# Cached attention in a hybrid decoder step: VectorE adds a page's scores ahead of, not behind, the low part of the page two later

## The chip, the cores and the metric

One NeuronCore of one Trainium2 chip runs the whole program. The metric is the device time of one execution in microseconds (us); the figure given for a kernel is the median of its runs.

## The reference

One inference step of a two-layer trunk, in float32: layer 0 is multi-head latent attention followed by a gated MLP, layer 1 is an S5 state-space layer followed by the same kind of MLP. The change lies in layer 0, in the attention of eight sample sequences with four new tokens each over a paged cache of 4096 positions (32 cache pages of 128 rows for each sequence):

```python
def one_sequence(a):
    pt, q1, c1, r1 = a
    c_all = jnp.concatenate([ckv_pool[pt].reshape(past, KV_LORA).astype(c1.dtype), c1], axis=0)
    r_all = jnp.concatenate([kpe_pool[pt].reshape(past, QK_ROPE).astype(r1.dtype), r1], axis=0)
    k, v = mla_keys_values(c_all, r_all, *kv_w)
    return causal_attend(q1, k, v, q_pos, k_pos)
```

`mla_keys_values` multiplies a latent row (256 numbers) by `w_kv_up` for 8 heads, puts the shared rotary key beside each head's 64 numbers and divides each head's key by its root mean square. `causal_attend` is a softmax attention with scale 96 ** -0.5.

## The kernel before

The program runs one stage after another: projections, attention of the prompt, attention over the cache (`attend_cache`, some 535 us), output projection, then the MLP, the S5 layer and the second MLP. Each stage is a block in which every engine has its own written-out instruction stream, and semaphores order them. An engine takes its instructions strictly in the order in which they are written here, so the place of an instruction in the stream is the subject of this case.

In `attend_cache` the unit of work is one cache page: `b` counts sequences (0 to 7), `p` pages of a sequence (0 to 31), `n = 32 b + p` pages in all. Sequences 0, 1, 6 and 7 are written out with constants, sequences 2 to 5 run in a loop, where `b` lives in a register and semaphore targets are worked out from it. The products must keep float32 accuracy, so a page's transposed latent is split into a high part (`cT_hi`, rounded) and a low part (`cT_lo`, the rest), and three products replace one. For a page n the engines do:

- TensorE: `turn_page` (L1307) transposes page n + 1 into the buffer `tc`; then the page's twelve matmuls (L1343 and L1345) into `kn`, which hold the keys of all heads and, in the last 32 columns, the unscaled scores. `tc`, `kn`, `cT_hi`, `cT_lo` and `sq` have two buffers each, taken in turn. In the twelve matmuls the latent is the stationary operand, so a weight load of `cT_hi` or `cT_lo` comes before each. Before the twelve, TensorE waits for `cl_done` (`cT_lo` of page n is there), `sq_done` and `s_kept` (both of page n - 2: its `kn` buffer has been read by ScalarE and by VectorE). Behind the pages with p % 4 == 1 it transposes the rotary keys of the next group of four pages (L1317), behind those with p % 4 == 3 it makes their scores (L1322).
- ScalarE: `hi` (L1428) copies `tc` of page n, rounded, into `cT_hi`; then `squares` (L1435) squares the keys of page n - 2 out of `kn`; at some pages also a copy of the rotary scores (L1444), of the rotary keys (L1455), or a square root for a group (L1462).
- VectorE: `lo` (L1536) subtracts `cT_hi` from `tc` of page n into `cT_lo`; then `sums` of page n - 2: the add of its scores (L1545) and the sum of its squares (L1546); at p % 4 == 1 and 3 also the work on a finished group of four pages (L1567; L1573, L1577, L1579). Once for each sequence come further operations of the softmax (L1596 to L1622).

The helper `behind` gives a function page p - 2, or one of the last two pages of the sequence before.

Of the kernel before, what the change touches and what calls it, by code (L numbers as in the profile page):

```python
# [573 lines left out]
NG = DM // GC  # L574
# [515 lines left out]
def attend_cache(nc, io, consts, keep, o_new, w_out):  # L1090
# [12 lines left out]
    GP = 4  # L1103
    EP = (NPAGE + 1) // 3
    NG = NPAGE // GP
# [3 lines left out]
    with ExitStack() as ctx:  # L1109
# [6 lines left out]
        def sem(name):  # L1116
            return ctx.enter_context(nc.semaphore("ca_" + name))
# [68 lines left out]
        sr_kept = sem("sr_kept")  # L1186
# [32 lines left out]
        def stream(b, page, at):  # L1219

            for p in range(NPAGE):
                if not isinstance(b, int) or b < NSEQ:
                    page(b, p)
                if p in at:
                    at[p](b)

        def behind(work, b, p):

            if p >= 2:
                work(b, p - 2)  # L1230
            elif not isinstance(b, int) or b > 0:
                work(b - 1, NPAGE - 2 + p)
# [260 lines left out]
        def _(dve):  # L1493
# [30 lines left out]
            def put_queries(b):  # L1524

                if not isinstance(b, int) or b >= 2:
                    dve.wait_ge(page_done, (b - 1) * NPAGE)
                nc.vector.tensor_copy(wb_hi[:, b % 2, :, HALF:], qc[:, :, b, :]).then_inc(q_put, 1)
                nc.vector.tensor_tensor(wb_lo[:, b % 2, :, HALF:], qc[:, :, b, :], qc_hi[:, :, b, :], ALU.subtract).then_inc(q_put, 1)

            def lo(b, p):
                n = b * NPAGE + p
                dve.wait_ge(ch_done, n + 1)
                if not isinstance(n, int) or n >= 2:
                    dve.wait_ge(page_done, n - 1)
                nc.vector.tensor_tensor(cT_lo[:, p % 2, :], tc[:, p % 2, 0:KVL], cT_hi[:, p % 2, :], ALU.subtract).then_inc(cl_done, 1)  # L1536

            def sums(b, p):
                n = b * NPAGE + p
                g = b * NG + p // GP  # L1540
                dve.wait_ge(sq_done, n + 1)

                dve.wait_ge(sr_kept, g + 1)
                cur = scores[:, b % 2, p, :]
                nc.vector.tensor_tensor(cur, cur, kn[:, p % 2, 1, HALF:HALF + QC], ALU.add).then_inc(s_kept, 1)  # L1545
                nc.vector.tensor_reduce(ssum[:, b % 2, p, :], sq[:, p % 2, :].rearrange("p (h d) -> p h d", h=H),  # L1546
                                        AXX, ALU.add).then_inc(ss_done, 1)
                if p % GP == 0:

                    dve.wait_ge(kpe_sqd, g + 1)  # L1550
                    nc.vector.tensor_reduce(ssum_pe[:, b % 2, p:p + GP], kpe_sq[:, p // GP % RG, :, :], AXX, ALU.add).then_inc(kpe_ss, 1)

            def page(b, p):
                if p == 0:
                    put_queries(b)
                lo(b, p)
                behind(sums, b, p)
                if p % GP == 1 and p > GP:
                    group_square(b, p // GP - 1)
                if p % GP == 3 and p > GP:  # L1560
                    scale_group(b, p // GP - 1)

            def group_square(b, g):

                own = slice(g * GP, (g + 1) * GP)
                dve.drain()
                nc.vector.tensor_tensor(rms[:, 0, g % 2, :, :], ssum[:, b % 2, own, :],  # L1567
                                        ssum_pe[:, b % 2, own].unsqueeze(2).to_broadcast([P, GP, H]), ALU.add).then_inc(ms_done, 1)

            def scale_group(b, g):  # L1570

                dve.wait_ge(sd_done, b * NG + g + 1)
                nc.vector.reciprocal(rms[:, 2, g % 2, :, :], rms[:, 1, g % 2, :, :])  # L1573
                dve.drain()
                cur = scores[:, b % 2, g * GP:(g + 1) * GP, :]
                flat = cur.rearrange("p g (h t) -> p (g h) t", h=H)
                nc.vector.tensor_tensor(flat, flat, rms[:, 2, g % 2, :, :].rearrange("p g h -> p (g h)").unsqueeze(2).to_broadcast([P, GP * H, NDEC]), ALU.mult)  # L1577
                dve.drain()
                nc.vector.tensor_reduce(tops[:, g, :], cur.rearrange("p g c -> p c g"), AXX, ALU.max)  # L1579
# [25 lines left out]
            def shift(b, part):  # L1605
                if in_range(b, 1, NSEQ):
                    dve.wait_ge(top_spread, b)
                    own = slice(0, NPAGE // 2) if part == 0 else slice(NPAGE // 2, NPAGE + 1)
                    cur = scores[:, (b - 1) % 2, own, :]
                    nc.vector.tensor_tensor(cur, cur, misc[:, 0:QC].unsqueeze(1).to_broadcast([P, own.stop - own.start, QC]), ALU.subtract).then_inc(shifted, 1)  # L1610
# [12 lines left out]

            def step(b):
                if isinstance(b, int) and b == NSEQ:
                    behind(sums, b, 0)
                    behind(sums, b, 1)
                stream(b, page, {1: begin, 3: last_group, 4: mean, 5: column_top, 9: row_top,
                                 12: lambda b: shift(b, 0), 13: lambda b: shift(b, 1)})

            sequences(dve, step)
            dve.wait_ge(o_done, 1)
            nc.vector.tensor_copy(o_new[:, :], kn[0:TS, 0, 0, :]).then_inc(o_kept, 1)
# [1661 lines left out]
```

## Time and profile before

| | |
|---|---|
| median of 3 runs | 3077.82 us |
| range of the runs | 3076.28 to 3091.57 us |
| the profiled execution | 3089.39 us |
| its span, first to last instruction | 3087.6 us |
| mean granted TensorE clock, share of full | 0.975 |
| TensorE busy (matmuls) | 2940.7 us, 95% of the span |
| VectorE busy | 1871.4 us, 61% |
| ScalarE busy | 968.2 us, 31% |
| first matmuls of the cached stage, its first and last page | 434.3 and 962.2 us |

The profile records one execution. PE is TensorE's matmuls, PEld its weight loads, which overlap the matmuls; DVE is VectorE, ACT ScalarE, POOL GpSimd. A row's line number is that of the code above. "Idle before" is the time that an engine stood still right ahead of an instruction, with the instruction whose semaphore ended it. Busy shares over the whole span mix stages with different limits; the cached stage is about a sixth of it.

### The profile page before, as it was taken

How to read it: one execution, taken by the hardware profiler on the slowest of the kernel's cores; microseconds unless marked ns; L12 is line 12 of the kernel's file. 1: busy time of each engine (PE TensorE's matmuls, PEld its weight loads, DVE VectorE, ACT ScalarE, POOL GpSimd, SP SyncE). 2: the span in 40 equal slices, each digit the busy share in tenths (PEclk: the TensorE clock that was granted, in tenths of full speed). 3: DMA queues.
4: the chain of work that ended last, by engine and by line, in shares of the span. 5: the costliest groups of instructions: out<-in, count | busy, mean ns of one | idle time of the engine just before them, and what ended most of it. 6: DMA issues, size and time to landing. Idle time of an engine off the chain costs nothing. (4 is left out here: it accounts for less than half of the span.)

```text
span 3087.6 us, 54484 instructions
## 1 busy us (share of the span) xinstructions
PE 2940.7 (95%) x19232; PEld 2756.5 (89%) x19232; DVE 1871.4 (61%) x3827; ACT 968.2 (31%) x1739; POOL 266.9 (9%) x352
## 2 busy tenths in 40 slices
PE   8979889999998999999999998999989999999998
PEld 5646679998996899999999987989989999999998
DVE  3436667777775465656665675882346556666565
ACT  3433345555554322222222232222222222222221
POOL 1003300000000000000000007650000000000000
PEclk9988999999998999999999998989999999999999
DMA  3010013222221021111111124334111111111111
GB/s 110 28 23 1 35 45 82 73 75 70 74 75 46 28 62 42 41 49 46 48 41 54 35 73 116 80 105 126 42 51 60 44 41 43 52 48 41 54 34 69
DMA packets 262263, 174.37 MB, mean 56 GB/s; under 512 B 77977, under 2 KB 247658, under 8 KB 261818
## 3 DMA queue, kind: packets, MB, share of 16 engines
q1 hardware_dynamic: 261882, 171.85, 19.3%
q8 instruction: 102, 1.67, 0.2%
q14 instruction: 87, 0.71, 0.1%
q10 hardware_dynamic: 192, 0.13, 0.0%
HBM read 149.49 MB, written 22.29 MB: 56 GB/s over the span
## 5 line engine op out<-in xcount | busy, mean ns | idle before, releaser
L1641 PE MATMUL f_up<-h_hi,f_wu_hi 128*128 128x352 f32 x2112 | 459.8, 326 | 16.8 <-DVE h_lo L2145 15.1
L1641 PE MATMUL f_up<-h_hi,f_wu_lo 128*128 128x352 f32 x2112 | 457.1, 324 | 0.0
L1641 PE MATMUL f_up<-h_lo,f_wu_hi 128*128 128x352 f32 x2112 | 456.9, 325 | 0.0
L1641 PEld LDWEIGHTS f_up<-h_hi,f_wu_hi 128*128 128x128 f32 x2112 | 361.2, 190 | 18.0 <-issue 15.7
L1641 PEld LDWEIGHTS f_up<-h_hi,f_wu_lo 128*128 128x128 f32 x2112 | 364.5, 189 | 0.0
L1641 PEld LDWEIGHTS f_up<-h_lo,f_wu_hi 128*128 128x128 f32 x2112 | 360.6, 189 | 0.0
L2053 ACT ACTIVATE f_conv<-f_u_row,f_taps 128x1056 f32<-128x1056 f32 x88 | 111.8, 1271 | 774.2 <-DVE f_u_row L2175 774.2
L2244 DVE TENSOR_TENSOR resid<-resid,f_down 128x352 f32<-128x352 f32 x528 | 271.3, 518 | 107.2 <-PE f_down L1999 104.1
L2175 DVE TENSOR_TENSOR f_u_row<-f_up,inv 128x1056 f32<-128x1056 f32 x88 | 110.5, 1256 | 345.0 <-PE f_up L1641 331.9
L1999 PE MATMUL f_down<-f_a_hi,f_wd_hi 128*128 (+1 forms) x960 | 317.1, 330 | 1.1 <-DVE resid L2244 0.5
L1999 PE MATMUL f_down<-f_a_hi,f_wd_lo 128*128 (+1 forms) x960 | 309.7, 323 | 0.0
L1999 PE MATMUL f_down<-f_a_lo,f_wd_hi 128*128 (+1 forms) x960 | 309.3, 322 | 0.0
L1999 PEld LDWEIGHTS f_down<-f_a_hi,f_wd_hi 128*128 128x128 f32 x960 | 180.3, 188 | 16.4 <-DVE resid L2244 9.1
L2191 DVE SCALAR_TENSOR_TENSOR f_conv<-f_u_row,f_taps,f_conv 128x512 f32<-128x512 f32 x176 | 126.0, 748 | 106.4 <-ACT f_u_new L2055 106.4
L1999 PEld LDWEIGHTS f_down<-f_a_lo,f_wd_hi 128*128 128x128 f32 x960 | 181.0, 188 | 0.0
L1999 PEld LDWEIGHTS f_down<-f_a_hi,f_wd_lo 128*128 128x128 f32 x960 | 180.6, 188 | 0.0
L1546 DVE TENSOR_REDUCE ca_ssum<-ca_sq 128x8 f32<-128x512 f32 x256 | 173.7, 678 | 0.0
L1343 PE MATMUL ca_kn<-ca_wa_hi,ca_cT_hi 128*128 128x256 f32 x512 | 158.0, 324 | 14.3 <-DVE ca_scores L1545 14.3
L1536 DVE TENSOR_TENSOR ca_cT_lo<-ca_tc,ca_cT_hi 128x256 fp32r<-128x256 f32 x256 | 107.8, 421 | 97.3 <-ACT ca_cT_hi L1428 93.3
L1435 ACT ACTIVATE ca_sq<-ca_kn 128x512 f32<-128x512 f32 x256 | 152.6, 596 | 1.5 <-PE ca_kn L1345 1.5
L1345 PE MATMUL ca_kn<-ca_wb_hi,ca_cT_lo 128*128 128x288 f32 x512 | 140.9, 298 | 0.0
L1428 ACT ACTIVATE ca_cT_hi<-ca_tc 128x256 fp32r<-128x256 f32 x256 | 97.7, 382 | 137.8 <-PE ca_tc L1307 134.8
(428 smaller groups left out, 5628.1 us busy)
## 6 DMA issues: line engine op xcount, KB each, us to landing
f_wu<-ffn_w_up SPq DMA_DIRECT2D x86, 512.0 KB, 4.0
ca_cache<-cache_ckv SPq DMA_DIRECT2D x256, 128.0 KB, 2.0
raw<-ffn_w_down SPq DMA_DIRECT2D x44, 512.0 KB, 4.2
raw<-ssm_w_out SPq DMA_DIRECT2D x16, 512.0 KB, 3.8
s_spill<-resid SPq DMA_DIRECT2D x8, 528.0 KB, 10.7
s_u<-sm_ut SPq DMA_DIRECT2D x8, 528.0 KB, 2.7
resid<-s_spill SPq DMA_DIRECT2D x8, 528.0 KB, 8.5
pj_xb<-x_prompt SPq DMA_DIRECT2D x8, 512.0 KB, 3.6
```

Of the source, the lines that this page charges most:

```text
L1343: nc.tensor.matmul(kn[:, p % 2, 0, 0:HALF], c[:, p % 2, k * P:(k + 1) * P], wa[:, k, :], start=(x == 0 and k == 0), stop=(x == 2 and k == ...
L1345: mm = nc.tensor.matmul(kn[:, p % 2, 1, 0:HALF + QC], c[:, p % 2, k * P:(k + 1) * P], wb[:, s, k, :], start=(x == 0 and k == 0), stop=(x = ...
L1428: nc.scalar.activation(cT_hi[:, p % 2, :], tc[:, p % 2, 0:KVL], ACT.Copy).then_inc(ch_done, 1)
L1435: nc.scalar.activation(sq[:, p % 2, :].rearrange("p (a c) -> p a c", a=2), kn[:, p % 2, :, 0:HALF], ACT.Square).then_inc(sq_done, 1)
L1536: nc.vector.tensor_tensor(cT_lo[:, p % 2, :], tc[:, p % 2, 0:KVL], cT_hi[:, p % 2, :], ALU.subtract).then_inc(cl_done, 1)
L1546: nc.vector.tensor_reduce(ssum[:, b % 2, p, :], sq[:, p % 2, :].rearrange("p (h d) -> p h d", h=H), AXX, ALU.add).then_inc(ss_done, 1)
L1641: mm = nc.tensor.matmul(out(c), w, x(c), start=(first and n == 0), stop=(last and n == 2))
L1999: mm = nc.tensor.matmul(down[:, x % 2, 0:CH], w[:, jj, m * P:(m + 1) * P], a[:, chunk(c)], start=(jj == 0 and q == 0), stop=(jj == GJ - 1 ...
L2053: nc.scalar.activation(conv[:, half, :], u_row[:, half, 2:], ACT.Identity, bias=taps[:, 3, bass.ds(t, 1)], scale=taps[:, 2, bass.ds(t, 1)])
L2175: nc.vector.tensor_tensor(u_row[:, half, 2:].rearrange("p (c n) -> p c n", c=NCH), up[:, half, :, 0:CH], inv[:, :].rearrange("p (c n) -> p ...
L2191: nc.vector.scalar_tensor_tensor(out=c[:, own], in0=u_row[:, half, own.start + 1:own.stop + 1], scalar=w[1], in1=c[:, own], op0=ALU.mult, ...
L2244: nc.vector.tensor_tensor(cur, cur, down[:, x % 2, 0:CH], ALU.add).then_inc(added, 1)
```

## The change

`sums` is cut in two. Its first half, the wait for the squares and for the rotary scores and the add of the scores, becomes `latent_scores`, which `page` calls for page p - 2 ahead of `lo` for page p. The rest of `sums` stays behind `lo`. Behind the last page the two halves run for each of the two pages left. No operation is added or taken away and no semaphore changes its meaning.

```diff
-            def sums(b, p):
+            def latent_scores(b, p):
                 n = b * NPAGE + p
-                g = b * NG + p // GP
                 dve.wait_ge(sq_done, n + 1)
-
-                dve.wait_ge(sr_kept, g + 1)
+                dve.wait_ge(sr_kept, b * NG + p // GP + 1)
                 cur = scores[:, b % 2, p, :]
                 nc.vector.tensor_tensor(cur, cur, kn[:, p % 2, 1, HALF:HALF + QC], ALU.add).then_inc(s_kept, 1)
+
+            def sums(b, p):
+                g = b * NG + p // GP
                 nc.vector.tensor_reduce(ssum[:, b % 2, p, :], sq[:, p % 2, :].rearrange("p (h d) -> p h d", h=H),
                                         AXX, ALU.add).then_inc(ss_done, 1)
                 if p % GP == 0:
@@ -1553,6 +1554,7 @@
             def page(b, p):
                 if p == 0:
                     put_queries(b)
+                behind(latent_scores, b, p)
                 lo(b, p)
                 behind(sums, b, p)
                 if p % GP == 1 and p > GP:
@@ -1623,8 +1625,9 @@
             def step(b):
                 if isinstance(b, int) and b == NSEQ:
-                    behind(sums, b, 0)
-                    behind(sums, b, 1)
+                    for p in range(2):
+                        behind(latent_scores, b, p)
+                        behind(sums, b, p)
```

## Rows read from the trace of the kernel before

**Rows 1.** The stage's middle, by stretches: busy us of each engine, clock, DMA share

```profile
core 0: us, PE busy (x) PEld busy (x) DVE busy (x) ACT busy (x) POOL busy (x), PEclk, DMA share, GB/s
...
620.00:680.00 60.00, 58.20 (x499) 54.88 (x498) 45.94 (x135) 33.28 (x86) 2.94 (x7) 1.00 0.28 71
```

**Rows 2.** Who waited for whom, TensorE, 434 to 970 us: total, times, longest

```profile
PEld ca_kn L1343 <- DVE ca_cT_lo L1536: 15.8, 18, 1.3
...
PE ca_kn L1343 <- DVE ca_scores L1545: 14.3, 22, 1.2
```

**Rows 3.** Groups by line, 434 to 970 us: busy, mean ns, idle before

```profile
L1536 DVE TENSOR_TENSOR ca_cT_lo<-ca_tc,ca_cT_hi 128x256 fp32r<-128x256 f32 x256 | 107.8, 421 | 97.3 <-ACT ca_cT_hi L1428 93.3
...
L1428 ACT ACTIVATE ca_cT_hi<-ca_tc 128x256 fp32r<-128x256 f32 x255 | 97.3, 382 | 137.8 <-PE ca_tc L1307 134.8 <-issue 2.1
```

**Rows 4.** Timeline around page 23 of sequence 3: start, duration

```profile
675.93 0.37 ACT L1428 ACTIVATE ca_cT_hi<-ca_tc 128x256 fp32r<-128x256 f32 x1
...
676.19 0.60 ACT L1435 ACTIVATE ca_sq<-ca_kn 128x512 f32<-128x512 f32 x1
...
676.34 0.42 DVE L1536 TENSOR_TENSOR ca_cT_lo<-ca_tc,ca_cT_hi 128x256 fp32r<-128x256 f32 x1 [0.43 <-ACT ca_cT_hi L1428]
...
676.83 0.19 DVE L1545 TENSOR_TENSOR ca_scores<-ca_scores,ca_kn 128x32 f32<-128x32 f32 x1
...
676.93 0.68 DVE L1546 TENSOR_REDUCE ca_ssum<-ca_sq 128x8 f32<-128x512 f32 x1
676.95 0.26 PEld L1307 LDWEIGHTS ca_tc<-ident,ca_cache 128*128 128x128 f32 x2
...
677.17 0.19 PEld L1343 LDWEIGHTS ca_kn<-ca_wa_hi,ca_cT_hi 128*128 128x128 f32 x1
```

**Rows 5.** The same timeline, on to page 24 of the sequence

```profile
677.53 0.34 DVE L1573 RECIPROCAL ca_rms<-ca_rms 128x32 f32<-128x32 f32 x1
...
678.31 0.39 DVE L1579 TENSOR_REDUCE ca_tops<-ca_scores 128x32 f32<-128x128 f32 x1
...
678.62 0.41 DVE L1536 TENSOR_TENSOR ca_cT_lo<-ca_tc,ca_cT_hi 128x256 fp32r<-128x256 f32 x1
...
678.95 0.17 DVE L1545 TENSOR_TENSOR ca_scores<-ca_scores,ca_kn 128x32 f32<-128x32 f32 x1
...
679.24 0.19 PEld L1343 LDWEIGHTS ca_kn<-ca_wa_hi,ca_cT_hi 128*128 128x128 f32 x1
```

**Rows 6.** The same timeline, on to page 25 of the sequence

```profile
679.70 0.59 ACT L1435 ACTIVATE ca_sq<-ca_kn 128x512 f32<-128x512 f32 x1
...
680.97 0.19 PEld L1343 LDWEIGHTS ca_kn<-ca_wa_hi,ca_cT_hi 128*128 128x128 f32 x1
```

**Rows 7.** Timeline at page 19 of sequence 3, behind ScalarE's work on exponentials and root

```profile
664.56 0.59 ACT L1435 ACTIVATE ca_sq<-ca_kn 128x512 f32<-128x512 f32 x1
...
665.18 0.19 DVE L1545 TENSOR_TENSOR ca_scores<-ca_scores,ca_kn 128x32 f32<-128x32 f32 x1
...
665.48 0.19 PEld L1343 LDWEIGHTS ca_kn<-ca_wa_hi,ca_cT_hi 128*128 128x128 f32 x1 [1.33 <-DVE ca_cT_lo L1536]
```

**Rows 8.** Squares and add at page 22 of sequence 3 (in the loop)

```profile
674.21 0.59 ACT L1435 ACTIVATE ca_sq<-ca_kn 128x512 f32<-128x512 f32 x1
...
674.92 0.19 DVE L1545 TENSOR_TENSOR ca_scores<-ca_scores,ca_kn 128x32 f32<-128x32 f32 x1 [0.15 <-ACT ca_sq L1435]
```

**Rows 9.** The same pair at page 18 of sequence 6 (written out)

```profile
865.64 0.59 ACT L1435 ACTIVATE ca_sq<-ca_kn 128x512 f32<-128x512 f32 x1
...
866.27 0.19 DVE L1545 TENSOR_TENSOR ca_scores<-ca_scores,ca_kn 128x32 f32<-128x32 f32 x1
```

**Rows 10.** Stretches around the one fall of the clock inside the stage

```profile
691.00:697.60 6.60, 3.36 (x26) 2.89 (x24) 3.06 (x11) 2.45 (x7) 0.40 (x1) 0.91 0.30 82
697.60:704.40 6.80, 6.57 (x34) 6.58 (x34) 3.64 (x12) 1.39 (x5) 0.00 (x0) 0.59 0.32 85
704.40:720.00 15.60, 15.60 (x131) 15.58 (x130) 13.29 (x40) 8.94 (x25) 0.80 (x2) 1.00 0.22 58
```

## The prediction

> **What bounds the kernel now.** I read the page's busy line first (TensorE's matmuls fill 95% of the span), then the stretches, waits and groups of the cached stage alone, and last its timeline page by page, since the change moves one small instruction by one place. In 60 us of the stage's middle TensorE's matmuls are busy for 58.20 us at the full clock and VectorE for 45.94 us [rows 1]: TensorE sets the pace and VectorE has about a quarter of its time free, but not at every moment. What counts is the moment at which a cache page's twelve matmuls may start. I take it from the weight load L1343 that opens them.
>
> The waits of TensorE [rows 2] name two things: the weight load stood 15.8 us for `cT_lo` and the matmul 14.3 us for `ca_scores`. These are the same pauses seen on two queues. The timeline tells which of the two came last: at page 23 of sequence 3 the low part had ended at 676.76, the add ended at 677.02, the weight load began at 677.17 [rows 4]; at page 24 the add ended at 679.12 and the load began 0.12 later at 679.24 [rows 5]; at page 19 it is 665.37 and 665.48, 0.11 later [rows 7]. So where TensorE waits today it waits for the add, the later of VectorE's two instructions, and 0.11 us is the way from such an end to the load. At page 23 it did not wait: its transposes (from 676.95, 0.26) had only just ended.
>
> The second thing to see is what VectorE waits for. Ahead of `lo` it stands 97.3 us in all, 93.3 of them for `cT_hi` [rows 3]. Ahead of the add it hardly stands, because `lo` fills the time. On ScalarE `hi` of page n comes first and `squares` of page n - 2 right behind it: 675.93 and 676.19, ending at 676.30 and 676.79 [rows 4]. The squares therefore end about 0.49 us after the high part, and the add starts 0.04 after them (676.83), or 0.03 at page 19 [rows 4, 7]. `lo` of page 23 started at 676.34, 0.04 after its high part, while the squares were still running.
>
> **The change part by part.** It adds and removes no operation and issues no transfer. It moves one add of 0.19 us (256 of them) ahead of `lo` and with it the wait for the squares. Behind that waiting instruction now stand `lo` of page n, the reduction of page n - 2 and all group work; for `lo` waits TensorE. No other queue is passed: SyncE's loads wait for `page_done` and have a DMA share of 0.28 to move in [rows 1], POOL's squares of the rotary keys wait for nothing that moves.
>
> *A page whose add waits for the squares.* Two consecutive VectorE instructions start closer than the first one's duration: add to the next 0.10 (676.83 to 676.93) [rows 4], `lo` to the next 0.33 (678.62 to 678.95) [rows 5]. The new order at page 23: add at 676.83 as before, `lo` 0.10 later at 676.93, its end 0.42 later at 677.35, the weight load 0.11 later at 677.46 instead of 677.17 [rows 4]: 0.29 us late. In short, the load can start no sooner than 0.67 after the squares' end (0.04 + 0.10 + 0.42 + 0.11), where it was 0.38 after. At page 19, where ScalarE is late, the load moves from 665.48 to 665.18 + 0.63 = 665.81, 0.33 late [rows 7].
>
> *The next page, with the group's work on VectorE.* The reduction now starts 0.33 behind `lo`, at 677.26 instead of 676.93, 0.33 late. From there to `lo` of page 24 it was 1.69 us of work without a gap (676.93 to 678.62) [rows 4, 5]. The new order has the add at 678.95, `lo` at 679.05, its end (0.41) at 679.46, the load 0.11 later at 679.57 instead of 679.24: 0.33 late in all, so this page adds 0.04. Where VectorE is behind anyway, the swap itself costs 0.01: `lo` then add took 0.50 from start to end, add then `lo` takes 0.51.
>
> *The page after it.* Page 25's squares ended at 680.29 and its load began at 680.97, 0.68 after [rows 6]. That is just the 0.67 needed, and ScalarE's squares move by 0.29 with the matmuls of page 23 while the load moves by 0.33, so nothing is added. The pages with p % 4 == 2 may be held up by about 0.1, but the page behind them is held more and by a chain that starts one page earlier (its high part is made from a transpose issued ahead of the wait), so the larger of the two counts, not the sum.
>
> *The sum.* One group of four pages loses 0.33 us. There are 8 groups in a sequence and 8 sequences: 64 x 0.33 = 21.1 us. The groups are not all alike. Behind exponentials the wait is the 0.33 of page 19; some groups have more room. I take 0.33 as the mean.
>
> *The loop.* In sequences 2 to 5 a wait's target is worked out in a register first. Where a new value is wanted right at the add, the add starts late: squares' end 674.80, add 674.92, 0.12 after [rows 8], against 866.23 and 866.27, 0.04 after, at the written-out sequence 6 [rows 9]. Today `lo`'s own targets are worked out while the reduction runs. In the new order they stand between a waiting add and `lo`, with nothing to cover them. No row shows this; from below it costs nothing, from above the step of rows 8 once or twice (0.08 to 0.16) on each held page. I take 0.12 for each group: 4 sequences x 8 groups x 0.12 = 4 us.
>
> The forecast is 21 + 4 = 25 us. Against the profiled execution that is 3089.4 + 25 = 3114 us; that execution lies 12 us above the median of the runs, and the difference carries over: 3077.8 + 25 = 3103 us.
>
> *The bounds.* From below: if a quarter of the groups have the room and the page behind adds nothing, 48 x 0.29 = 14 us. From above: if the reduction had to wait for all of `lo` (0.42 instead of 0.33), 64 x 0.09 = 6 us more; if the register step is also paid in the written-out sequences, 4 more; if pages with p % 4 == 1, which have 0.01 to spare, pay the step in full, 0.1 x 64 = 6 more: 41 us.
>
> *A rule weighed.* Rows 4 show the reduction starting 0.10 behind an add that lasts 0.19. The Trainium skill, page "VectorE: DVE Perf Modes", section "The DRAIN you can't avoid", says that the next operation does not start until the pipeline has emptied; a later section ("Two Vector instructions with no wait between them") says that one that is not held starts earlier. By the first, `lo` would start 0.19 behind the add and the reduction 0.42 behind `lo`, 0.09 more at both places: 0.18 x 64 = 11.5 us on top, 3115 us. The trace agrees with the second, and the sum goes by its rows.
>
> **The rivals.**
> - *Hidden (no change).* The whole stage has DVE and ACT idle time, and VectorE's order could be free. For it: only 22 waits for the add are recorded, so most pages have some room. Against it: the room is 0.15 us between the add's end and the load at page 23 [rows 4], of which 0.11 is the way itself, and the new end lies 0.33 later than the old one. It would need the squares to end 0.3 us sooner. A half-size version (only pages with late squares lose, many groups have room) gives 10 to 15 us, 3088 to 3093 us, inside what can be told from no change.
> - *Faster.* `s_kept` comes sooner at pages where VectorE is behind, such as page 24: the add would end at 678.62 + 0.17 instead of 679.12 [rows 5]. If that were the gate and `lo` were not needed at once, all waits for the add would go: 14.3 us [rows 2], 3063 us. It decides only if the first weight load could start without `lo`; but the twelve matmuls wait for both ahead of the first load, and `lo` ends later by the same work.
> - *The clock.* TensorE has more short pauses. The one fall inside the stage came behind a stretch with 3.36 us busy of 6.60 [rows 10]; the pause of 1.33 us at page 19 [rows 7] lies in a stretch with the clock at full [rows 1]. In the fall's 6.80 us 34 matmuls ran, where at full clock 131 took 15.60 [rows 10], so 57 would have run: 23 x 0.119 = 2.7 us lost. If the pauses, now up to 1.33 + 0.33, cause one such fall in each of 7 sequences, 19 us come on top: 3122 us. The Trainium skill, page "TensorE: Matmul & The Clock Gate", section "A second HAM failure mode: psum-queue depth-cycling", says that frequent small pauses between matmul groups can make the clock swing; no row here shows that for pauses of this size.
> - *VectorE falls behind for good.* If the idle time ahead of the add plus group work exceeded a page's period, delays would add up: 0.1 us on each of 256 pages gives 26 us on top, 3129 us. Against it: page 25 shows VectorE back on time.
>
> **How the numbers follow.** A measurement of this kernel tells from no change what is over about 0.5%, 15 us. Chances: forecast mechanism at its size or near (18 to 40 us slower) 0.70; half-size or hidden 0.18; clock 0.05; falling behind 0.03; faster 0.04. The likeliest one's own range is 3093 to 3119 us. To hold 8 in 10, the range goes from 3085 (part of the half-size cases) to 3122 (the clock's case). Slower by over 0.5%: 0.70 + 0.05 + 0.03 = 0.78; within 0.5%: 0.19; faster 0.03, since that case reaches only 14.3 us.
>
> **What would show it.** In the profile after: VectorE's idle time ahead of `lo` for `cT_hi` is nearly gone, and an idle time of the same order or more (100 to 140 us) stands ahead of the add, ended by `ca_sq`; TensorE waits for `ca_cT_lo` ahead of L1343 and no longer for `ca_scores`, some 100 times or more and some 50 us in total; the load of L1343 starts 0.67 after the squares' end at pages 3, 7, ..., 31, and 0.1 to 0.2 more in sequences 2 to 5. The stage from 434.3 to 962.2 us grows by 25 us and the other stages by nothing. It would be wrong if squares end relatively sooner than now, if the clock falls more often in the stage, or if pages with p % 4 == 1 and 2 are held as well.

## The result and the profile after

The changed kernel takes 3104.81 us (median of 8 runs, 3099.72 to 3109.75) against 3079.61 us (8 runs, 3074.77 to 3091.57) for the one before. The ratio is 1.0081, with a 95% interval of 1.0067 to 1.0094: 0.81% slower, 21 to 29 us. The profiled execution took 3109.75 us, its span is 3107.9 us.

The stage itself can be told more closely than the whole. From the first to the last page's opening weight load it lasts 548.7 us (433.9 to 982.6) instead of 527.9 (434.3 to 962.2): 20.8 us more. What is left of the span is 2559.2 us after and 2559.7 before, so in this pair nothing else moved. Over the twelve executions profiled in this case, the rest of the span lies anywhere from 2539.7 to 2559.7 us although its code is the same; that spread, and not the stage, makes the medians uneven. It goes with the mean granted clock of the execution: the shortest rest, 2539.7 us, has 0.982, the longest, 2559.7 us, 0.975. For each kernel below both numbers are given, and the stage is what its explanation goes by. Each stage figure is one profiled execution against the one of the kernel before (527.9 us); the change, profiled a second time in a later session, gave 21.8 us instead of 20.8, so a difference of 1 us between such figures tells nothing.

Who waited for whom in the changed kernel, 434 to 1000 us; total, times, longest:

```profile
PEld ca_kn L1343 <- DVE ca_cT_lo L1536: 24.1, 48, 1.6
...
DVE ca_scores L1543 <- ACT ca_sq L1435: 134.7, 174, 5.0
...
DVE ca_cT_lo L1536 <- ACT ca_cT_hi L1428: 1.1, 1, 1.1
```

VectorE's idle time has changed its place. It stood 93.3 us for the high part ahead of `lo` [rows 3]; now that is 1.1 us, and 134.7 us stand ahead of the add, for the squares. TensorE's matmul waits of 14.3 us for the scores [rows 2] are gone from the list; what it waits for is the low part (its matmuls 15.2 us).

Page 23 of sequence 3 in the changed kernel, the counterpart of [rows 4]:

```profile
685.04 0.37 ACT L1428 ACTIVATE ca_cT_hi<-ca_tc 128x256 fp32r<-128x256 f32 x1
...
685.31 0.60 ACT L1435 ACTIVATE ca_sq<-ca_kn 128x512 f32<-128x512 f32 x1
...
685.94 0.19 DVE L1543 TENSOR_TENSOR ca_scores<-ca_scores,ca_kn 128x32 f32<-128x32 f32 x1 [0.51 <-ACT ca_sq L1435]
...
686.10 0.42 DVE L1536 TENSOR_TENSOR ca_cT_lo<-ca_tc,ca_cT_hi 128x256 fp32r<-128x256 f32 x1
...
686.20 0.26 PEld L1307 LDWEIGHTS ca_tc<-ident,ca_cache 128*128 128x128 f32 x2
686.45 0.67 DVE L1547 TENSOR_REDUCE ca_ssum<-ca_sq 128x8 f32<-128x512 f32 x1
686.58 0.19 PEld L1343 LDWEIGHTS ca_kn<-ca_wa_hi,ca_cT_hi 128*128 128x128 f32 x1
```

The high part ends at 685.41, as early as ever, but `lo` starts at 686.10. The squares end at 685.91, the add starts 0.03 later, `lo` 0.16 after the add, and it ends at 686.52; TensorE is through with its transposes by 686.46 and begins only at 686.58.

The same page of sequence 6, which is written out with constants and not in the loop:

```profile
898.33 0.60 ACT L1435 ACTIVATE ca_sq<-ca_kn 128x512 f32<-128x512 f32 x1
898.96 0.19 DVE L1543 TENSOR_TENSOR ca_scores<-ca_scores,ca_kn 128x32 f32<-128x32 f32 x1 [0.68 <-ACT ca_sq L1435]
899.07 0.42 DVE L1536 TENSOR_TENSOR ca_cT_lo<-ca_tc,ca_cT_hi 128x256 fp32r<-128x256 f32 x1
...
899.54 0.19 PEld L1343 LDWEIGHTS ca_kn<-ca_wa_hi,ca_cT_hi 128*128 128x128 f32 x1 [0.19 <-DVE ca_cT_lo L1536]
```

Here `lo` starts 0.11 behind the add, and the load 0.61 behind the squares' end (898.93) instead of 0.67. From `lo`'s end to the load it is 0.05.

The growth by sequence, from the starts of the pages' opening weight loads (from the last page of the sequence before to its own last page), after minus before, in us:

| sequence | 0 | 1 | 2 | 3 | 4 | 5 | 6 | 7 |
|---|---|---|---|---|---|---|---|---|
| | 2.05 | 2.05 | 3.41 | 3.03 | 3.03 | 3.23 | 2.00 | 2.02 |

The written-out sequences lose 2.03 us each, those in the loop 3.18. By a page's place in its group of four, the period that ends with a page of p % 4 == 3 has 11.8 us of the growth, p % 4 == 0 3.3, p % 4 == 2 4.1 (3.6 of them in the loop) and p % 4 == 1 1.5.

### The profile page after: what moved, and what is told of

The parts are those of the page before. It is cut to its first block and busy times, and to the rows that moved or that the text cites. A ratio compares the mean times of both kernels' runs of the same rounds, so it can differ in the third digit from the quotient of the medians.

```text
span 3107.9 us, 54484 instructions
## 1 busy us (share of the span) xinstructions
PE 2958.4 (95%) x19232; PEld 2759.2 (89%) x19232; DVE 1865.0 (60%) x3827; ACT 968.9 (31%) x1739; POOL 266.1 (9%) x352
## 5 line engine op out<-in xcount | busy, mean ns | idle before, releaser
L1644 PE MATMUL f_up<-h_hi,f_wu_hi 128*128 128x352 f32 x2112 | 459.6, 326 | 16.8 <-DVE h_lo L2148 15.2
L1343 PE MATMUL ca_kn<-ca_wa_hi,ca_cT_hi 128*128 128x256 f32 x512 | 162.0, 331 | 15.8 <-DVE ca_cT_lo L1536 15.2
L1345 PE MATMUL ca_kn<-ca_wb_lo,ca_cT_hi 128*128 128x288 f32 x512 | 140.8, 297 | 0.0
```

Of the source, the lines that this page charges most:

```text
L1343: nc.tensor.matmul(kn[:, p % 2, 0, 0:HALF], c[:, p % 2, k * P:(k + 1) * P], wa[:, k, :], start=(x == 0 and k == 0), stop=(x == 2 and k == ...
L1345: mm = nc.tensor.matmul(kn[:, p % 2, 1, 0:HALF + QC], c[:, p % 2, k * P:(k + 1) * P], wb[:, s, k, :], start=(x == 0 and k == 0), stop=(x = ...
L1644: mm = nc.tensor.matmul(out(c), w, x(c), start=(first and n == 0), stop=(last and n == 2))
```

## The experiments

Each kernel was timed in five rounds beside the kernel before, on the same chip as that one. There were three such sessions, each on a chip of its own: e1 to e4; e5 to e8; the change again and e9. Ratios are to the kernel before of the same session; stages are all compared with the 527.9 us above.

**Where the loss sits: e1_new_at_3 and e2_new_but_3.** The new order at one page in four, then at the other three:

```diff
# e1_new_at_3
-                behind(latent_scores, b, p)
+                if p % GP == 3:
+                    behind(latent_scores, b, p)
                 lo(b, p)
+                if p % GP != 3:
+                    behind(latent_scores, b, p)
                 behind(sums, b, p)
# e2_new_but_3: the same with == and != exchanged
```

> The new order at the pages with p % 4 == 3 alone, the old order at the other three in four. Theory of the prediction (the low part now stands behind an add that waits for the squares, and the pages whose squares end late have no room): these pages and the group pages behind them carried 12.3 + 3.3 us of the change's 20.8 us in the stage, and some of what the loop's p % 4 == 2 pages took comes back to them, so 15 to 19 us slower than before. Rival, that the new order costs about the same at every page: a quarter, 5 to 7 us.

> The new order at all pages but those with p % 4 == 3. Theory of the prediction: only page 16 of a sequence (0.28 us late, 7 times) and, in the looped sequences, the pages that are held by the register step (about 0.12 at each p % 4 == 2) lose, 6 to 9 us slower than before. Rival of an even cost: three quarters, 16 to 19 us.

(The 12.3 us in the expectation of e1 should read 11.8.) e1 measured 1.0057 (1.0043 to 1.0070), 18 us, stage + 19.4 us, a little over its band. e2 measured 1.0014 (1.0005 to 1.0023), 4 us, stage + 5.4 us. One page in four carries nearly the whole loss; the even split (5 to 7 and 16 to 19 us) falls. e2 came out under its band (6 to 9 us) by time and by stage. In it, page 16 is 0.17 late in written-out sequences and 0.25 in the loop, where 0.28 had been written down. That the two add up to more than the change (24.8 against 20.8 us) is also as it should be: a page held at p % 4 == 2 costs nothing where the page behind is held anyway.

**Wait or place: e3_wait_alone.** The old order of operations, with one wait more:

```diff
+                behind(squares_made, b, p)     # dve.wait_ge(sq_done, n + 1) of that page
                 lo(b, p)
                 behind(sums, b, p)
```

> The old order of the operations, and one more wait: VectorE waits for the squares of page n - 2 ahead of the low part of page n. Nothing else moves. Theory of the prediction: it is the wait and not the place of the add that costs, so the time is about that of the change, 18 to 30 us slower than before, and TensorE waits for the add, about 0.6 to 0.7 us after the squares' end. Rival, that the add's own 0.10 us ahead of the low part, or another order of writes, is what costs: no change, within 5 us of before.

1.0093 (1.0079 to 1.0106), 29 us, stage + 29.0 us. Page 23 of sequence 6:

```profile
906.42 0.60 ACT L1435 ACTIVATE ca_sq<-ca_kn 128x512 f32<-128x512 f32 x1
907.05 0.42 DVE L1539 TENSOR_TENSOR ca_cT_lo<-ca_tc,ca_cT_hi 128x256 fp32r<-128x256 f32 x1 [0.68 <-ACT ca_sq L1435]
...
907.39 0.17 DVE L1548 TENSOR_TENSOR ca_scores<-ca_scores,ca_kn 128x32 f32<-128x32 f32 x1
...
907.68 0.19 PEld L1343 LDWEIGHTS ca_kn<-ca_wa_hi,ca_cT_hi 128*128 128x128 f32 x1 [0.23 <-DVE ca_cT_lo L1539]
```

No operation has been moved, and the loss is all there. `lo` starts 0.03 behind the squares' end (907.02), the add ends at 907.56, the load comes 0.12 later, 0.66 behind the squares. (The row puts the pause down to `cT_lo`, which had ended at 907.47; the add was the last.) The wait is the cause. The add's place is even the better one once the wait stands: the way from the squares' end to the load is 0.05 longer here than in the changed kernel.

The 29.0 us are not the price of the wait alone, though. The written-out sequences lose 2.67 us each (2.03 in the changed kernel), the looped ones 4.59 (3.18). Page 23 of sequence 3, in the loop:

```profile
689.72 0.60 ACT L1435 ACTIVATE ca_sq<-ca_kn 128x512 f32<-128x512 f32 x1
690.51 0.42 DVE L1539 TENSOR_TENSOR ca_cT_lo<-ca_tc,ca_cT_hi 128x256 fp32r<-128x256 f32 x1 [0.68 <-ACT ca_sq L1435]
...
691.14 0.19 PEld L1343 LDWEIGHTS ca_kn<-ca_wa_hi,ca_cT_hi 128*128 128x128 f32 x1 [0.23 <-DVE ca_cT_lo L1539]
```

Here `lo` starts 0.19 behind the squares' end (690.32) and the load 0.82 behind it, so the added wait brings 0.16 more in the loop. The clean comparison is that of the written-out sequences.

**The loop's surplus: e4_targets_first and e9_squares_named_first.** In e4 both waits of `lo` are put ahead of the add's two waits, so that nothing is left to do between a waiting add and `lo`; ScalarE makes the high part before the squares in any case.

```diff
# e4_targets_first
+                lo_ready(b, p)          # lo's waits: ch_done n + 1, page_done n - 1
                 behind(latent_scores, b, p)
                 lo(b, p)                # without waits
# e9_squares_named_first, on top of e4: the wait for sq_done ahead of lo_ready
+                behind(squares_made, b, p)
                 lo_ready(b, p)
                 behind(latent_scores, b, p)   # with the wait for sr_kept alone
```

> The change, with the low part's own two waits (high part made, matmuls of page n - 2 done) put ahead of the add's waits, so that in the looped sequences nothing is worked out between a waiting add and the low part. Theory: the looped sequences lose 3.07 us each and the written-out ones 2.1; with this they lose alike, 3 to 4.5 us less than the change, 20 to 22 us slower than before, and the low part starts 0.10 after the add everywhere. Rival, that the loop's surplus comes from something else: the time of the change, 24 to 26 us slower.

1.0099 (1.0084 to 1.0115), 31 us: slower than the change, not faster. Stage + 33.7 us. Half of the theory holds and half does not. The sequences now lose alike (4.6, 4.0, 4.6, 4.2, 4.2, 4.4, 3.8, 3.9 us), and `lo` starts 0.10 to 0.11 behind the add everywhere, so what stood between a waiting add and `lo` did make the surplus at the held pages. What is left of it, 0.3 us a sequence, lies at the first page of a looped sequence. But the level is that of the loop's sequences and more, 2 us over the change in each written-out one, because the add itself starts late:

```profile
908.53 0.60 ACT L1435 ACTIVATE ca_sq<-ca_kn 128x512 f32<-128x512 f32 x1
909.33 0.19 DVE L1545 TENSOR_TENSOR ca_scores<-ca_scores,ca_kn 128x32 f32<-128x32 f32 x1 [0.68 <-ACT ca_sq L1435]
```

The squares end at 909.13 and the add starts 0.20 later, at the same page where it was 0.03 in the changed kernel. The new theory was that the order in which the waits are written decides which of them travels with the instruction.

> The change itself once more, so that the next kernel can be compared with it on the same chip: 22 to 28 us slower than before.

> The low part's waits ahead of the add, as in e4, but the wait for the squares is written first of all of them. In e4 the add started 0.20 after the squares' end instead of 0.03. Theory: only the first wait written ahead of an instruction travels with it, the others are steps of the engine's sequencer that cost some 0.17 once the late one is through; with the squares written first the add starts 0.03 to 0.05 after them again, the low part 0.10 after the add in the looped sequences too, and the time is 3 to 5 us under the change, 20 to 22 us slower than before. Rival, that the number of waits costs whatever their order: as e4, 30 us slower.

On the third chip the change measured 1.0067 (1.0050 to 1.0084), 21 us and so just under its band of 22 to 28, with a stage of + 21.8 us, and e9 1.0071 (1.0045 to 1.0098), 22 us (14 to 30), with + 27.2 us. By time the two can't be told apart, and e9's lies in its band; by the stage e9 is 5.4 us worse than the change and 6.5 better than e4 (on another chip), and that misses the band. By sequence e9 lost 2.4, 2.1, 4.7, 4.6, 4.6, 4.5, 2.3, 2.0 us. Page 23 of sequence 3 (loop), then that of sequence 6 (written out), both of e9:

```profile
690.83 0.60 ACT L1435 ACTIVATE ca_sq<-ca_kn 128x512 f32<-128x512 f32 x1
691.65 0.19 DVE L1546 TENSOR_TENSOR ca_scores<-ca_scores,ca_kn 128x32 f32<-128x32 f32 x1 [0.62 <-ACT ca_sq L1435]
691.75 0.42 DVE L1538 TENSOR_TENSOR ca_cT_lo<-ca_tc,ca_cT_hi 128x256 fp32r<-128x256 f32 x1
...
907.37 0.60 ACT L1435 ACTIVATE ca_sq<-ca_kn 128x512 f32<-128x512 f32 x1
908.00 0.19 DVE L1546 TENSOR_TENSOR ca_scores<-ca_scores,ca_kn 128x32 f32<-128x32 f32 x1 [0.68 <-ACT ca_sq L1435]
908.11 0.42 DVE L1538 TENSOR_TENSOR ca_cT_lo<-ca_tc,ca_cT_hi 128x256 fp32r<-128x256 f32 x1
```

Written out, the add starts 0.03 behind the squares (907.97, 908.00) although four waits stand ahead of it, two of them those of `lo`: the order in which the waits are written is what counts, not their number, and the rival falls for these sequences. In the loop it starts 0.22 behind (691.43, 691.65), and the forecast of an even loss fails there. The likely reason is that in the loop the next thing behind the first-named wait is not the add but the step that works out a target in a register, and that this step takes the wait; that is inferred from the starts (`lo` in e3 starts 0.19 instead of 0.03 behind in the same way) and was not tried by itself. An order that is good in both kinds of sequence stays unfound.

**ScalarE's order: e5_squares_first, e6_squares_first_old and e7_mixed.** The squares end late because ScalarE makes the high part first. Here that is turned round, under the new order on VectorE (e5), under the old one (e6), and, with the new order, everywhere but at the pages with p % 4 == 3, which keep the old order on both engines (e7).

```diff
# e5_squares_first (on the change), e6_squares_first_old (on the kernel before)
-                hi(b, p)
                 behind(squares, b, p)
+                hi(b, p)
# e7_mixed: squares first and scores first if p % GP != 3, both behind hi and lo if p % GP == 3
```

> The change, and ScalarE squares page n - 2 ahead of the high part of page n (it did the reverse). The add then waits for squares that end early, and the low part for a high part that starts some 0.05 later at most pages, since the squares fill the time of the transposes. Theory: the chain squares, add, low part is cut; only the pages with p % 4 == 3 and page 16 lose, where the high part is late already (it moves by 0.49, the load by about 0.12), and the group page behind adds 0.05: 9 to 14 us slower than before, about half of the change. Rival, that ScalarE's order does not matter and the add's place does: 24 to 26 us slower.

> The kernel before, and ScalarE squares first, as a control: with the old order on VectorE the load needs the high part, the low part and the add in turn. Theory: at p % 4 == 3 the high part is 0.49 later, the add then ends 0.50 after the low part's start, the load comes about 0.25 to 0.3 late: 16 to 24 us slower than before, more than with the new order on VectorE. Rival, that whichever order ScalarE takes is free: within 5 us of before.

> Squares first on ScalarE and the add first on VectorE, but both in the old order at the pages with p % 4 == 3. Theory: every page then has its chain inside its period; page 16 is 0.17 late in seven sequences; 0 to 4 us slower than before, hardly to be told from it. Rival, that the add ahead of the low part costs by itself: 8 us slower or more (three quarters of the pages carry it).

| | ratio | interval | stage |
|---|---|---|---|
| e5 | 1.0036 | 1.0023 to 1.0050 | + 11.1 us |
| e6 | 1.0062 | 1.0049 to 1.0075 | + 19.0 us |
| e7 | 0.9993 | 0.9984 to 1.0002 | + 0.1 us |

All three lie in their bands by the stage (e7's time even lies 2 us under the kernel before, not to be told from it). Page 23 of sequence 3 in e5:

```profile
677.34 0.59 ACT L1435 ACTIVATE ca_sq<-ca_kn 128x512 f32<-128x512 f32 x1
...
677.82 0.38 ACT L1428 ACTIVATE ca_cT_hi<-ca_tc 128x256 fp32r<-128x256 f32 x1
...
677.96 0.19 DVE L1543 TENSOR_TENSOR ca_scores<-ca_scores,ca_kn 128x32 f32<-128x32 f32 x1 [0.99 <-ACT ca_sq L1435]
...
678.23 0.42 DVE L1536 TENSOR_TENSOR ca_cT_lo<-ca_tc,ca_cT_hi 128x256 fp32r<-128x256 f32 x1
...
678.71 0.19 PEld L1343 LDWEIGHTS ca_kn<-ca_wa_hi,ca_cT_hi 128*128 128x128 f32 x1
```

Now the add has its squares at 677.93, ahead of the high part (678.20), and `lo` follows the high part by 0.03: the chain is cut. What is left is the high part's own delay of 0.48 by the squares, which a page of this kind has no room for. Its load comes 0.12 late in e5 and 0.28 in e6 at most pages with p % 4 == 3 that had none to spare (0.17 and 0.34 at page 19). At those pages the looped sequences lose what the written-out ones lose, save at page 31 (0.17 against 0.12): an add that does not wait hides the register step, which bears out from the other side what the loop's surplus was. e7 shows the add ahead of `lo` at three pages in four with no loss at any but page 16 (0.17, as written down) and the first page of a looped sequence (0.13 to 0.25), and a gain of 0.05 to 0.07 at pages 20, 24 and 28. So the add's new place costs next to nothing where ScalarE squares first. ScalarE's mixed order with the old order on VectorE was not tried, so e7 doesn't tell what the add's place gives or takes by itself.

**A faster kernel: e8_pair_early.** On the kernel before:

```diff
# ScalarE
                 hi(b, p)
-                behind(squares, b, p)
+                if p % GP != 3:
+                    behind(squares, b, p)
+                if p % GP == 2:
+                    behind(squares, b, p + 1)
# VectorE
+                if p % GP == 3:
+                    behind(sums, b, p)
                 lo(b, p)
-                behind(sums, b, p)
+                if p % GP != 3:
+                    behind(sums, b, p)
```

> An attempt at a faster kernel from the same rows. At pages with p % 4 == 2 ScalarE squares the two pages n - 2 and n - 1, ahead of the group's root; VectorE at p % 4 == 3 does the whole of page n - 2 (add and reduction) ahead of the low part, in the idle time that it has there. VectorE then starts the group's work some 0.6 us sooner and the pages with p % 4 == 0, which wait 0.10 to 0.12 for it today, no longer wait: 3 to 8 us faster than before. Rival: the high part behind two squares comes too late and the pages with p % 4 == 3 are held: 5 to 20 us slower.

0.9980 (0.9969 to 0.9991), 6 us faster, stage - 5.4 us. Page 23 of sequence 3, the counterpart of [rows 4] and the first row of [rows 5]:

```profile
676.36 0.19 DVE L1548 TENSOR_TENSOR ca_scores<-ca_scores,ca_kn 128x32 f32<-128x32 f32 x1 [0.16 <-ACT ca_sq L1435]
...
676.46 0.68 DVE L1549 TENSOR_REDUCE ca_ssum<-ca_sq 128x8 f32<-128x512 f32 x1
...
677.06 0.41 DVE L1539 TENSOR_TENSOR ca_cT_lo<-ca_tc,ca_cT_hi 128x256 fp32r<-128x256 f32 x1
...
677.39 0.34 DVE L1579 RECIPROCAL ca_rms<-ca_rms 128x32 f32<-128x32 f32 x1
...
677.53 0.19 PEld L1343 LDWEIGHTS ca_kn<-ca_wa_hi,ca_cT_hi 128*128 128x128 f32 x1
```

VectorE does the add and the reduction in what was idle time, and the group's work starts at 677.39, ahead of the page's load; before, it began 0.36 behind it (677.53 and 677.17 in [rows 5, 4]). The pages with p % 4 == 0 gain 0.10 to 0.16 where they had waited and the first page of a sequence 0.5, the pages with p % 4 == 3 give back 0.05 to 0.07.

## Why the prediction was right

- *The whole.* Forecast 25 us (3103), measured 25.2 (3104.81), interval 21 to 29. The profiled pair grew by 20.4 us. So the agreement to 0.2 us is partly luck; the stage's own 20.8 us is 4 under the sum, and the second measurement of the change gave 21 us (15 to 26).
- *The mechanism.* Named as the wait that `lo` would stand behind: shown by e3 (the wait added and nothing moved; 2.67 us for a written-out sequence against 2.03 in the changed kernel, + 29.0 us in all) from one side and by e5 and e7 (the wait gone or short, + 11.1 and + 0.1) from the other.
- *The held page: the term that was mis-sized.* Predicted 0.67 from the squares' end to the load, so 0.29 late at page 23; measured 0.61 in the written-out sequences, 0.23 late. The 0.11 from an operation's end to the load had been read from the add; behind `lo` it is 0.05. The add's start (0.04) and the spacings (0.10 and 0.42) were right within 0.01 there. At the very page that was worked out, in sequence 3, the load does come 0.67 behind the squares, but by two errors that cancel: `lo` starts 0.16 behind the add instead of 0.10, and the load 0.06 behind `lo` instead of 0.11.
- *The page behind.* Predicted 0.04 more; measured 0.04 at pages 24 and 28 (0.05 in the loop). Group: 0.27 instead of 0.33. With groups that have more room (page 7 loses 0.05 to 0.08) and those that have less (page 19 0.27, page 8 up to 0.16), a sequence loses 2.03 instead of 2.64 us: the 21.1 us term is 16 us.
- *The loop.* Predicted 0.12 for each group, 4 us in all; measured (3.18 - 2.03) x 4 = 4.6 us. It is made up otherwise than was taken: `lo` starts only 0.06 later behind a waiting add (0.16 to 0.17 against 0.11), at a dozen pages of a sequence, and the first page of a looped sequence loses 0.30 more than that of a written-out one (`lo` starts 0.20 to 0.43 behind the add there, against 0.10). The pages with p % 4 == 2 are late by 0.13 there, but the page behind is then late by 0.16 instead of 0.23: the larger of the two counts, as predicted.
- *What the profile was to show.* Idle time ahead of the add of 100 to 140 us: 134.7. None for the high part: 1.1. TensorE waiting for `cT_lo`: yes, but 48 times and 24.1 us, not over 100 times and 50 us; most of the new pauses are so short that the list of waits leaves them out, and the loads' starts had to be compared page by page. The load was to start 0.67 behind the squares' end, and 0.1 to 0.2 more in the loop: it was 0.61, and 0.06 to 0.07 more. The stage was to grow by 25 us: 20.8.
- *A sign of being wrong that did come.* Pages with p % 4 == 1 and 2 were not to be held as well. They are, in part: 1.5 and 4.1 us of the 20.8, most of it in the loop, where at p % 4 == 2 the load comes 0.78 behind the squares' end. There the add itself starts 0.12 behind them, the step of [rows 8], against 0.03 in the written-out sequences. It costs little in the sum, because the page behind is held anyway.
- *The clock.* The stage has one fall of the clock in it, as before; the mean is 0.976 against 0.975. That rival did not come.
- *The emptied pipeline.* `lo` starts 0.11 behind an add of 0.19 in the written-out sequences, so the reading of [rows 4] holds. The Trainium skill, page "VectorE: DVE Perf Modes", section "The DRAIN you can't avoid", says that the next operation does not start until the pipeline is empty, but also that one that is not held starts earlier, and for what holds one it points to its section "Two Vector instructions with no wait between them". The trace agrees with the second statement; by the first alone, `lo` would have started 0.19 behind the add. In the loop it is 0.16 to 0.17 for another reason: with `lo`'s waits ahead of the add (e4) it is 0.10 to 0.11 there too.

## What to carry to other kernels

Ask of an instruction that is moved ahead not how long it is but what it waits for, and what is behind it on its engine: 0.19 us of work cost up to 0.27 us a page, because it brought a wait for the last of another engine's two results ahead of the one result that the bottleneck needs. The new order was free only where the producer's order was turned round with it and a page had room for that (e7, not e5), and an idle stretch ahead of a waiting instruction is the place for work whose inputs can be made early (e8). Where a loss is spread over a few tenths at some pages, compare the starts of one recurring instruction page by page; lists of waits and medians of whole runs are too coarse.

## What was not expected of the hardware

- From the end of an operation to the weight load that it releases it was 0.11 to 0.12 us for the add in the kernel before and 0.05 to 0.06 for the low part in the changed one. That the place of the wait among TensorE's three waits makes the difference is a guess.
- An instruction with several waits started 0.03 us behind the last release or 0.20 to 0.22 behind it, by the order in which the waits were written (e4, e9): 0.17 us for the same waits, and in a loop with targets in registers the order that gave 0.03 outside gave 0.22 (e9).
- The rest of the program, some 2550 us of unchanged code, differed by up to 20 us between single executions on several chips, the shorter ones at the higher mean granted clock.
